# One-hot scatter in one-pass products, and the last block's down units at the head of the next pair

## The chip, the cores and the metric

The kernel runs on one core of one Trainium2 chip. The metric is the device time of one execution in microseconds (us), lower is better. Three runs of the kernel before gave a median of 1330.48 us, from 1329.83 to 1330.93.

## The reference

A two-layer transformer trunk for 256 tokens of width 1024, in float32. Each layer has a mixer (causal pooling and mLSTM heads), a layer norm, a channel mixer and another layer norm. The channel mixer of layer 0 is a dense SwiGLU; that of layer 1 picks two of eight experts for each token. The change lies in this last part:

```python
def moe_swiglu(x, w_router, b_router, wg, wu, wd):
    logits = (x @ w_router) + b_router
    top_v, top_i = lax.top_k(logits, 2)
    top_w = jax.nn.softmax(top_v, axis=-1)
    combine = jnp.sum(jax.nn.one_hot(top_i, 8) * top_w[..., None], axis=-2)
    out = jnp.zeros_like(x)
    for e in range(8):
        out = out + combine[..., e:e + 1] * ((silu(x @ wg[e]) * (x @ wu[e])) @ wd[e])
    return out
```

wg and wu are 1024 x 3584 per expert and wd is 3584 x 1024. All of them are read once: 336 MiB for this layer.

## The kernel before, in words

**Precision.** A matmul of float32 operands is two instructions in the trace; one of operands rounded to a short format (float32r) is one, called a one-pass matmul here. A product that has to be as exact as float32 is made of several one-pass matmuls: each weight unit is rounded by ScalarE into w_hi (L821) and VectorE writes the rest into w_lo (L1177). Tokens are split into high and low parts in the same way.

**Units.** The weights come as units of 128 x 2048 float32 (1 MiB), one DMA each on the sync engine's queue (SP), into a ring of nine slots (raw, arena and tokens memory). Four w_hi and three w_lo buffers follow. ScalarE rounds three units ahead of TensorE and VectorE subtracts two ahead, in the order of the units; a buffer comes free when TensorE is done with the unit in it (unit_done).

**Pairs.** The experts are sorted by their number of tokens and worked on in four pairs. In a pair, stream A is an expert with up to 128 tokens, and a unit of it costs 12 matmuls of 512 columns (three passes, `product`, L1768). Stream B is an expert with up to 64 tokens; its high and low parts stand side by side in one 128-wide operand, and a unit costs 8 matmuls (`one_pass`, L2098). B's lower rows are then added to the upper ones: ScalarE copies them to `fold` (L1059), TensorE adds them with a shift matrix (`add_lower`, L2145). The hidden width of 3584 is cut into blocks 0, 1, 2 of 1024 and block 3 of 512. A pair has 84 units: for each block b the gates (g), the ups (u) of A and B and then the downs (d) of the block before. In a pair, "units 16 to 19" are the downs of block 3 of the pair before (LATE = 4 units), placed behind the gates and ups of block 0 (ROUND = 20). The first pair starts at unit 4.

**Around a block.** After the gates ScalarE applies silu (L1043); after the ups VectorE multiplies (L1637); TensorE turns the product (L2132 for A, L2139 for B); ScalarE rounds it into eh_hi or eh_n (L1048, L1054) and VectorE writes the rest (L1643, L1650). The next block's gates of the same stream wait for that, because they use the same PSUM banks (2, 3 for A, 6, 7 for B). The dictionaries in `Events` say at which unit of the pair each step stands in each engine's queue.

**Gather and scatter.** TensorE gathers tokens by products with one-hot matrices (L2073), behind units 75 to 81. For the scatter, VectorE writes masks "token t sits in slot s" times the token's weight (L1520, L1531), TensorE turns them behind unit 68 (L2217) and ScalarE copies them to `scat` (L1109), in float32. When the last downs are through, ScalarE copies the sums of A (banks 0, 1) and B (banks 4, 5) to y_a (L1101) and y_b (L1104). `scatter_pair` (L2095, L2096) multiplies `scat` and y in float32, behind units 22 and 23, and VectorE adds the four results to `work` (L1633), behind units 24 to 27.

**Loops.** Pair 0 and pair 3 are written out. Pairs 1 and 2 are one body in a hardware loop on each engine (`Fori(1, PAIRS - 1)`). An overflow body (`extra`) for experts with more tokens stands behind a branch on n_over, which is 0 here.

**The end.** After pair 3 come its own four down units of block 3, the last scatter into banks 2, 3, 6, 7 (L2285, L2292), four additions (L1633), each followed by a bn_stats (L1729), the aggregates (L1733), two square roots on ScalarE (L1164) and the scaled result (L1742, L1744).

Of the kernel before, what the change touches and what calls it, by code (L numbers as in the profile page):

```python
# [7 lines left out]
F32 = mybir.dt.float32  # L8
# [24 lines left out]
E = 8  # L33
# [111 lines left out]
class Events:  # L145


    def __init__(self, order, first):
# [4 lines left out]
        self.turn_a = {(v + 4 if b < EXP_BLOCKS - 1 else v + 3): b for v, b in self.up_a.items()}  # L153
        self.turn_b = {(v + 4 if first and b == 0 else v + 5): b for v, b in self.up_b.items()}
# [3 lines left out]
        self.read_a = {after[0][(b - 1) % EXP_BLOCKS]: b for b in range(1 if first else 0, EXP_BLOCKS)}  # L158
        self.read_b = {after[1][(b - 1) % EXP_BLOCKS]: b for b in range(1, EXP_BLOCKS)}
        self.read_b[max(self.turn_b, key=lambda v: -self.turn_b[v])] = 0  # L160
        if first:
            self.read_a[max(self.turn_a, key=lambda v: -self.turn_a[v]) + 2] = 0
# [51 lines left out]
def build(nc, x, w_in, b_gates, conv_w, conv_b, pool_w, pool_scale, mlstm_g, w_out, ln1_g, ln1_b, ln2_g, ln2_b,  # L214
          wg_dense, wu_dense, wd_dense, w_router, b_router, wg_exp, wu_exp, wd_exp, consts, out):
    with ExitStack() as ctx:
# [16 lines left out]
        parts = sb("parts", [P, 3 * (XG + EH) + EBLK + TT * P + P + TT * NARROW], F32R)  # L233
# [25 lines left out]
        def carve(shape, start=None):  # L259
            if start is not None:  # L260
# [70 lines left out]

        esg = carve([EBLK], 2048)
        esg_n = carve([EBLK])
        y_a = carve([D])
        pickc, pickc_n = (shaped(y_a[:, n * TT * P:(n + 1) * TT * P], [TT, P]) for n in range(2))
        scat = carve([2, T])
        gt, eq = (shaped(scat[:, n, 0:TT * E * E], [TT, E, E]) for n in range(2))
        item_tab = carve([MAX_ITEMS + 1, 5])
        item_cur = carve([4, 5])

        y_b = carve([D])
        tables_end = at[0]
        logit = carve([TT, E], tables_end - D)
# [23 lines left out]
        assert at[0] <= tables_end  # L367
# [52 lines left out]
            shift_zero, fold_zero = map(sem, ("small_ready", "gatew_zero", "gatew_ready", "pool_steps", "convp_ready",  # L420
                                    "pool_ready", "mask_ready", "tokens_ready", "shift_zero", "fold_zero"))
        shift_ready, turn_go, sel_ready = map(sem, ("shift_ready", "turn_go", "sel_ready"))
        ln_last_in, ysb_half, mean_ready = map(sem, ("ln_last_in", "ysb_half", "mean_ready"))
# [170 lines left out]
        def _(sp):  # L594
# [71 lines left out]
            def later_loads(p, last=False):  # L666
                *late, a, b = (order_at(bass.ds(p * 2 + n, 1) if not last else slice(p * 2 + n, p * 2 + n + 1))
                               for n in range(4))
                pair_loads(p, PAIR, lambda stream, kind, blk, v: late[stream == "B"] if ROUND - LATE <= v < ROUND else
# [38 lines left out]
        def _(pool):  # L708
# [5 lines left out]
            g.memset(fold[0:NARROW, :].bitcast(F32), 0.0).then_inc(fold_zero, 1)  # L714
# [93 lines left out]
        def _(act):  # L808
# [304 lines left out]
            def extra(j):  # L1113

                i = j + PAIRS
                for n in range(2):
# [35 lines left out]
            a.copy(y_a, wide_bank(SUM_A, D)).then_inc(ysa_ready, 1)  # L1152
            act.wait_ge(unit_done, done(PAIRS, LATE - 1))
            a.copy(y_b[:, 0:HALF], bank[SUM_B]).then_inc(ysb_ready, 1)
# [13 lines left out]
        def _(dve):  # L1168
# [349 lines left out]
            def wide_slots(to, slot_of, combine_of):  # L1518
# [825 lines left out]
```

## Time and profile before

| | |
|---|---|
| median of three runs | 1330.48 us |
| the profiled execution, its own time | 1330.71 us |
| its span in the trace | 1328.9 us |
| TensorE, VectorE, ScalarE busy | 96%, 85%, 70% of the span |
| granted TensorE clock, mean | 0.992 of full speed |
| moved by DMA | 425.18 MB, 320 GB/s over the span |

The span is what the trace covers, from the first instruction to the last; the execution's own time has 1.8 us more. The expert layer runs from about 446 to 1310 us. TensorE is named PE for matmuls and PEld for weight loads, which overlap them; VectorE is DVE, ScalarE is ACT. Matmuls are pipelined, and a matmul's duration in the trace is longer than the distance to the next; the distance of the weight loads is the better measure of pace.

### The profile page before, as it was taken

What the parts mean: (1) busy time and instruction counts of PE and PEld (TensorE: products, weight loads), DVE (VectorE), ACT (ScalarE), POOL (GpSimd) and SP (SyncE); (2) the same over time, 40 slices, a digit from 0 to 9 for tenths busy, and PEclk for the clock granted to TensorE, in tenths of its full rate; (3) what the DMA queues carried; (4) which work ended last, traced back from release to release, by engine and by line L of the source; (5) the groups of instructions that cost most, each with busy time, mean ns of one, the idle gap of its engine ahead of it and who ended that gap; (6) DMA issues with size and microseconds to landing.
All of it is one profiled execution on the core that took longest, in us unless ns stands there. A gap on an engine that the chain in (4) does not pass through costs nothing.

```text
span 1328.9 us, 17008 instructions
## 1 busy us (share of the span) xinstructions
PE 1271.3 (96%) x6161; PEld 1035.8 (78%) x6161; DVE 1128.6 (85%) x943; ACT 929.7 (70%) x746; POOL 91.3 (7%) x111
## 2 busy tenths in 40 slices
PE   7999999999998999999999999899999999999996
PEld 6987888888977778778877777787777787677774
DVE  5887644458988899999998999888999989899997
ACT  5555334445543788888887888787878889788883
POOL 2560000000840000000000000000000000000000
PEclk9999999999998999999999999999999999999998
DMA  9647555544452999999999999999999999999992
GB/s 318 223 137 245 185 186 187 186 152 157 159 187 92 339 381 377 395 399 405 409 408 407 379 410 394 408 407 409 351 385 407 397 408 409 409 391 394 398 406 103
DMA packets 133053, 425.18 MB, mean 320 GB/s; under 512 B 9008, under 2 KB 11344, under 8 KB 132960
## 3 DMA queue, kind: packets, MB, share of 16 engines
q1 hardware_dynamic: 131600, 420.21, 83.3%
q0 software_dynamic: 1216, 3.71, 0.9%
q8 instruction: 53, 0.87, 0.3%
q14 instruction: 40, 0.33, 0.1%
q10 hardware_dynamic: 144, 0.07, 0.0%
HBM read 422.91 MB, written 1.05 MB: 319 GB/s over the span
## 4 chain that ended last, share of the span: by engine, by line
PE 74%; DVE 14%; issue 7%; ACT 4%; DMA 0%; DVEq 0%; ACTq 0%
PE bank L1770 19%; PE bank L1772 18%; PE bank L1771 18%; DVE w_lo L1177 8%; PE bank L2099 6%; PE bank L2100 6%; DVE w_lo L1191 2%; PE bank L2145 1%; ACT w_hi L836 1%; PE bank L2132 1%; PE bank L2073 1%; PE bank L2095 1%; PE bank L2096 1%; DVE arena L1272 1%; ACT w_hi L821 1%
## 5 line engine op out<-in xcount | busy, mean ns | idle before, releaser
L1177 DVE TENSOR_TENSOR w_lo<-raw,w_hi 128x2048 fp32r<-128x2048 f32 x216 | 485.9, 2285 | 34.4 <-PE bank L1772 18.7
L821 ACT CAST w_hi<-raw 128x2048 fp32r<-128x2048 f32 x216 | 407.5, 1915 | 67.6 <-PE bank L1772 66.7
L1770 PE MATMUL bank<-w_hi,parts 128*128 128x512 f32 x824 | 330.5, 401 | 18.7 <-issue 7.2
L1772 PE MATMUL bank<-w_hi,parts 128*128 128x512 f32 x824 | 322.8, 392 | 0.0
L1771 PE MATMUL bank<-w_lo,parts 128*128 128x512 f32 x824 | 322.7, 392 | 0.0
L2099 PE MATMUL bank<-w_hi,parts 128*128 128x512 f32 x672 | 270.9, 403 | 9.0 <-ACT arena L1043 3.1
L2100 PE MATMUL bank<-w_lo,parts 128*128 128x512 f32 x672 | 263.4, 392 | 0.0
L1770 PEld LDWEIGHTS bank<-w_hi,parts 128*128 128x128 f32 x824 | 155.7, 189 | 61.7 <-issue 19.5
L1191 DVE TENSOR_TENSOR w_lo<-raw,w_hi 128x2048 fp32r<-128x2048 f32 x61 | 140.7, 2308 | 60.0 <-PE bank L1772 45.5
L1177 DVE TENSOR_TENSOR w_lo<-arena,w_hi 128x2048 fp32r<-128x2048 f32 x80 | 181.1, 2285 | 9.4 <-issue 5.2
L1772 PEld LDWEIGHTS bank<-w_hi,parts 128*128 128x128 f32 x824 | 155.6, 189 | 33.4
L1771 PEld LDWEIGHTS bank<-w_lo,parts 128*128 128x128 f32 x824 | 155.8, 189 | 30.8 <-issue 0.7
L2099 PEld LDWEIGHTS bank<-w_hi,parts 128*128 128x128 f32 x672 | 126.7, 189 | 54.0 <-DVE w_lo L1177 23.0
L836 ACT CAST w_hi<-raw 128x2048 fp32r<-128x2048 f32 x61 | 115.9, 1909 | 75.2 <-PE bank L1772 66.1
L821 ACT CAST w_hi<-arena 128x2048 fp32r<-128x2048 f32 x80 | 150.9, 1913 | 17.5 <-PE bank L2100 14.1
L2100 PEld LDWEIGHTS bank<-w_lo,parts 128*128 128x128 f32 x672 | 126.8, 189 | 25.3 <-issue 0.7
L1177 DVE TENSOR_TENSOR w_lo<-tokens,w_hi 128x2048 fp32r<-128x2048 f32 x40 | 91.4, 2286 | 2.8 <-ACT w_hi L821 2.3
L1770 PE MATMUL bank<-w_hi,x_hi 128*128 128x512 f32 (+1 forms) x224 | 85.3, 381 | 4.0 <-DVE w_lo L1191 3.9
L1772 PE MATMUL bank<-w_hi,x_lo 128*128 128x512 f32 (+1 forms) x224 | 84.8, 378 | 0.0
L1771 PE MATMUL bank<-w_lo,x_hi 128*128 128x512 f32 (+1 forms) x224 | 84.7, 378 | 0.0
L821 ACT CAST w_hi<-tokens 128x2048 fp32r<-128x2048 f32 x40 | 76.9, 1921 | 6.0 <-issue 4.4
L1770 PE MATMUL bank<-x_hi,w_hi 128*128 128x256 f32 x256 | 73.5, 287 | 1.4 <-ACT arena L922 1.4
(256 smaller groups left out, 1255.4 us busy)
## 6 DMA issues: line engine op xcount, KB each, us to landing
raw<-in_wu_exp SPq DMA_DIRECT2D x76, 1024.0 KB, 10.8
raw<-in_wg_exp SPq DMA_DIRECT2D x70, 1024.0 KB, 10.0
raw<-in_wd_exp SPq DMA_DIRECT2D x70, 1024.0 KB, 10.6
arena<-in_wd_exp SPq DMA_DIRECT2D x29, 1024.0 KB, 10.2
arena<-in_wg_exp SPq DMA_DIRECT2D x26, 1024.0 KB, 10.9
arena<-in_wu_exp SPq DMA_DIRECT2D x25, 1024.0 KB, 9.1
raw<-in_w_in SPq DMA_DIRECT2D x20, 1024.0 KB, 5.8
tokens<-in_wg_exp SPq DMA_DIRECT2D x16, 1024.0 KB, 11.6
```

The lines of the kernel that those rows point to most:

```text
L821: a.copy(to, ring[s]).then_inc(hi_ready, 1)
L836: a.copy(w_hi[:, n % HIGH, :], raw[:, n % RAW, :]).then_inc(hi_ready, 1)
L1177: v.tensor_tensor(low(n), ring[s], high(n).bitcast(F32), ALU.subtract).then_inc(lo_ready, 1)
L1191: v.tensor_tensor(w_lo[:, n % SPLIT, :], raw[:, n % RAW, :], w_hi[:, n % HIGH, :].bitcast(F32), ALU.subtract).then_inc(lo_ready, 1)
L1272: ins = v.scalar_tensor_tensor(out=acc, in0=zqk[:, c, j:j + T], scalar=par_col(("conv_w", j), l, c), in1=acc, op0=ALU.mult, op1=ALU.add)
L1770: mm(psum, left[0], right[0], start=first, stop=False)
L1771: mm(psum, left[0], right[1], start=False, stop=False)
L1772: return mm(psum, left[1], right[0], start=False, stop=last)
L2073: last = mm(bank[n][:, kk * BOTH:(kk + 1) * BOTH], parts_[:, t, k * P:(k + 1) * P], pick_both[:, t, :], start=t == 0, stop=t == TT - 1)
L2095: mm(psum, scat[:, 0, at_t], y_a[:, at_d], start=True, stop=False)
L2099: mm(psum, left, right[0], start=first, stop=False)
L2100: return mm(psum, left, right[1], start=False, stop=last)
```

## The change

The one-hot matrix for the scatter no longer holds the tokens' weights, so it is exact in the short format. The weights are applied to the sums when they leave PSUM, together with the split in a high and a low part: ScalarE writes the high part with a scaled activation, VectorE the low part (`sums_low`). The factor per slot comes from four small products behind the turned masks (bank 7, copied to slot_w). The scatter has four one-pass matmuls per quarter instead of two float32 ones.

The parts lie in the memory of the last block's hidden values (eh_hi, eh_lo, eh_n) and of `fold`. So the last block's downs must have been multiplied before block 0 of the next pair writes there: they move from units 16 to 19 to units 0 to 3. Everything of block 0 moves four units back. Block 0's turn of A moves from behind unit 15 to behind unit 17 and is read there; its turn of B moves from unit 20 to unit 22. The scatter moves to units 6 and 7, the additions to 8 to 11. `add_lower` uses the lower 64 rows of its operands only, and the memset of the others goes. At the end the scatter is written without a branch in front of it, its B part by column halves, and VectorE's branch over the overflow body now stands behind the four additions and in front of the bn_stats.

```diff
-        for stream, kind, blk in (("A", "g", b), ("B", "g", b), ("A", "u", b), ("B", "u", b), ("A", "d", before),
-                                  ("B", "d", before)):
+        work = [("A", "g", b), ("B", "g", b), ("A", "u", b), ("B", "u", b)]
+        downs = [("A", "d", before), ("B", "d", before)]
+        for stream, kind, blk in work + downs if b else downs + work:
...
-        self.turn_a = {(v + 4 if b < EXP_BLOCKS - 1 else v + 3): b for v, b in self.up_a.items()}
-        self.turn_b = {(v + 4 if first and b == 0 else v + 5): b for v, b in self.up_b.items()}
+        self.turn_a = {(v + 2 if not first and b == 0 else v + 4 if b < EXP_BLOCKS - 1 else v + 3): b
+                       for v, b in self.up_a.items()}
+        self.turn_b = {(v + 5 if b else v + 4 if first else v + 3): b for v, b in self.up_b.items()}
...
-LATE_A, LATE_B = ROUND - LATE // 2 - 1, ROUND - 1
-SCATTER = {ROUND + 2: (0, 1), ROUND + 3: (2, 3)}
-ADD = {ROUND + 4: 0, ROUND + 5: 1, ROUND + 6: 2, ROUND + 7: 3}
+LATE_A, LATE_B = LATE // 2 - 1, LATE - 1
+SCATTER = {LATE + 2: (0, 1), LATE + 3: (2, 3)}
+ADD = {LATE + 4: 0, LATE + 5: 1, LATE + 6: 2, LATE + 7: 3}
...
+        ya_hi, ya_lo, yb_hi = (x.rearrange("p k c -> p (k c)") for x in (eh_hi, eh_lo, eh_n))
+        yb_lo = fold
...
-            g.memset(fold[0:NARROW, :].bitcast(F32), 0.0).then_inc(fold_zero, 1)
...
+            def sums_high(to, sums, n, ready):
+
+                a.activation(to, sums, ACT.Identity, scale=slot_w[:, n:n + 1]).then_inc(ready, 1)
...
+                        if b == 0 and not first:
+                            act.wait_ge(scat_mm, 4 * p)
                         lower_rows(b, 0)
...
                     if v == LATE_A and not first:
-                        a.copy(y_a, wide_bank(SUM_A, D)).then_inc(ysa_ready, 1)
+                        act.wait_ge(unit_done, done(p, v))
+                        act.wait_ge(slotw_ready, p)
+                        sums_high(ya_hi, wide_bank(SUM_A, D), 0, ysa_ready)
                     if v == LATE_B and not first:
                         act.wait_ge(unit_done, done(p, v))
-                        a.copy(y_b, wide_bank(SUM_B, D)).then_inc(ysb_ready, 1)
+                        sums_high(yb_hi, wide_bank(SUM_B, D), 1, ysb_ready)
...
+                        a.copy(slot_w[:], bank[7][:, 0:2]).then_inc(slotw_ready, 1)
                         a.copy(scat.rearrange("p a t -> p (a t)"), bank[3]).then_inc(scat_ready, 1)
...
+            def sums_low(to, sums, n, hi, rounded, ready):
+
+                dve.wait_ge(*rounded)
+                v.scalar_tensor_tensor(out=to, in0=sums, scalar=slot_w[:, n:n + 1], in1=hi.bitcast(F32),
+                                       op0=ALU.mult, op1=ALU.subtract).then_inc(ready, 1)
...
+                    if u == LATE_A + 1 and not first:
+                        dve.wait_ge(slotw_ready, p)
+                        sums_low(ya_lo, wide_bank(SUM_A, D), 0, ya_hi, (ysa_ready, p), yal_ready)
+                    if u == LATE_B + 1 and not first:
+                        dve.wait_ge(fold_mm, 2 * EXP_BLOCKS * p)
+                        sums_low(yb_lo, wide_bank(SUM_B, D), 1, yb_hi, (ysb_ready, p), ybl_ready)
...
-            dve.wait_ge(unit_done, done(PAIRS, LATE - 1))
-            v.tensor_copy(y_b[:, HALF:], bank[SUM_B + 1]).then_inc(ysb_half, 1)
+            dve.wait_ge(slotw_ready, PAIRS)
+            sums_low(ya_lo, wide_bank(SUM_A, D), 0, ya_hi, (ysa_ready, PAIRS), yal_ready)
+            dve.wait_ge(fold_mm, 2 * EXP_BLOCKS * PAIRS)
+            for n in range(2):
+                c = slice(n * HALF, (n + 1) * HALF)
+                sums_low(yb_lo[:, c], bank[SUM_B + n], 1, yb_hi[:, c], (ysb_ready, PAIRS + n), ybl_ready)
             n_over = dve.value_load(order_int[0:1, MAX_ITEMS + 2:MAX_ITEMS + 3], min_val=0, max_val=MAX_OVER)
+            for k, q in enumerate((0, 2, 1, 3)):
+                add_scattered(tail_mm, k + 1, q, bank[TAIL_BANKS[q]])
             with dve.If(0 < n_over):
...
-                mm(psum, scat[:, 0, at_t], y_a[:, at_d], start=True, stop=False)
-                mm(psum, scat[:, 1, at_t], y_b[:, at_d], start=False, stop=True).then_inc(scattered, 1)
+                mm(psum, scat[:, 0, at_t], ya_hi[:, at_d], start=True, stop=False)
+                mm(psum, scat[:, 0, at_t], ya_lo[:, at_d], start=False, stop=False)
+                mm(psum, scat[:, 1, at_t], yb_hi[:, at_d], start=False, stop=False)
+                mm(psum, scat[:, 1, at_t], yb_lo[:, at_d], start=False, stop=True).then_inc(scattered, 1)
...
+                        for n, picks in enumerate((pickc, pickc_n)):
+                            for t in range(TT):
+                                weights = mm(bank[7][:, n:n + 1], picks[:, t, :], item_cur[:, n, TT + t:TT + t + 1],
+                                             start=t == 0, stop=t == TT - 1)
+                        weights.then_inc(st_mm, 1)
...
-    nc = bacc.Bacc("TRN2", target_bir_lowering=False, num_devices=1, dynamic_dma_scratch_size=8192)
+    nc = bacc.Bacc("TRN2", target_bir_lowering=False, num_devices=1, dynamic_dma_scratch_size=4096)
```

## Rows read from the trace of the kernel before

**Rows 1.** The page, busy us by engine, with shares of the span.
```profile
PE 1271.3 (96%) x6161; PEld 1035.8 (78%) x6161; DVE 1128.6 (85%) x943; ACT 929.7 (70%) x746; POOL 91.3 (7%) x111
```
**Rows 2.** The page, the chain that ended last, by engine.
```profile
PE 74%; DVE 14%; issue 7%; ACT 4%; DMA 0%; DVEq 0%; ACTq 0%
```
**Rows 3.** Windows, units 0-27 of pairs 1-3: length, PE, PEld, DVE, ACT, POOL, clock, DMA, GB/s.
```profile
640.75:716.61 75.86, 74.61 (x318) 57.26 (x316) 67.72 (x37) 61.56 (x40) 0.00 (x0) 1.00 1.03 409
863.60:941.01 77.41, 76.14 (x316) 58.34 (x316) 65.60 (x35) 60.14 (x38) 0.00 (x0) 0.98 1.00 396
1084.48:1160.35 75.87, 74.43 (x318) 57.27 (x316) 67.91 (x37) 61.63 (x40) 0.00 (x0) 1.00 1.03 409
```
**Rows 4.** Timeline of weight loads: start, duration, and idle before with its releaser.
```profile
674.79 0.19 PEld L2099 LDWEIGHTS bank<-w_hi,parts 128*128 128x128 f32 x1 [0.41 <-DVE w_lo L1177]
...
678.72 1.03 PEld L2132 LDWEIGHTS bank<-cst,arena 128*128 128x128 f32 x8
...
690.59 0.19 PEld L1770 LDWEIGHTS bank<-w_hi,parts 128*128 128x128 f32 x1 [1.50 <-DVE w_lo L1177]
...
699.55 0.41 PEld L2095 LDWEIGHTS bank<-arena 128*128 128x128 f32 x2
...
702.78 0.19 PEld L1770 LDWEIGHTS bank<-w_hi,parts 128*128 128x128 f32 x1 [0.24 <-issue]
...
722.50 0.19 PEld L1770 LDWEIGHTS bank<-w_hi,parts 128*128 128x128 f32 x1
...
727.94 0.19 PEld L2099 LDWEIGHTS bank<-w_hi,parts 128*128 128x128 f32 x1
...
863.60 0.19 PEld L1770 LDWEIGHTS bank<-w_hi,parts 128*128 128x128 f32 x1 [3.56 <-issue]
...
1300.56 0.19 PEld L1770 LDWEIGHTS bank<-w_hi,parts 128*128 128x128 f32 x1 [0.58 <-issue]
```
**Rows 5.** The same timeline, around one tile's router products.
```profile
401.48 1.98 PEld L1779 LDWEIGHTS bank<-rout_w,arena 128*128 128x128 f32 x16
403.38 0.19 PEld L1770 LDWEIGHTS bank<-w_hi,parts 128*128 128x128 f32 x1
```
**Rows 6.** Timeline of VectorE in pair 1.
```profile
672.45 11.09 DVE L1177 TENSOR_TENSOR w_lo<-raw,w_hi 128x2048 fp32r<-128x2048 f32 x5
...
706.21 2.29 DVE L1177 TENSOR_TENSOR w_lo<-raw,w_hi 128x2048 fp32r<-128x2048 f32 x1 [3.87 <-PE bank L1772]
...
711.47 2.29 DVE L1177 TENSOR_TENSOR w_lo<-raw,w_hi 128x2048 fp32r<-128x2048 f32 x1 [2.37 <-PE bank L2100]
```
**Rows 7.** Waits of ScalarE, 446 to 1310 us, the longest.
```profile
ACT w_hi L821 <- PE bank L1772: 57.9, 70, 1.4
```
**Rows 8.** Windows of 30 us in pair 1, columns as in Rows 3.
```profile
735.00:765.00 30.00, 29.81 (x138) 23.72 (x137) 29.28 (x17) 24.30 (x16) 0.00 (x0) 1.00 0.99 375
...
795.00:825.00 30.00, 29.80 (x140) 23.77 (x139) 29.54 (x17) 24.36 (x18) 0.00 (x0) 1.00 1.04 393
```
**Rows 9.** Groups of instructions by form, 640 to 1300 us: busy, mean ns.
```profile
L1643 DVE TENSOR_TENSOR parts<-bank,parts 128x512 fp32r<-128x512 f32 x21 | 13.6, 684 | 5.9 <-ACT parts L1048 5.9
...
L1637 DVE TENSOR_TENSOR arena<-arena,bank 128x1024 f32<-128x1024 f32 x9 | 11.0, 1220 | 2.0 <-PE bank L1772 2.0
...
L1043 ACT ACTIVATE arena<-bank 128x1024 f32<-128x1024 f32 x9 | 9.2, 1027 | 17.6 <-PE bank L1772 17.6
```
**Rows 10.** Timeline of ScalarE, then of VectorE, at the end.
```profile
1310.58 1.28 ACT L1155 ACT_TABLE_LOAD   x1
1311.87 0.29 ACT L1155 ACTIVATE hstd<-small 128x1 f32<-128x1 f32 x1
1313.57 1.28 ACT L1164 ACT_TABLE_LOAD   x1 [1.40 <-issue]
...
1314.27 0.69 DVE L1633 TENSOR_TENSOR work<-work,bank 128x512 f32<-128x512 f32 x1 [3.60 <-PE bank L2292]
...
1319.87 0.21 DVE L1733 BATCH_NORM_AGGREGATE mv<-stats 128x2 f32<-128x12 f32 x1
```

More of the change, by code:

```diff
@@ L330, in build @@
         xg_n, eh_n = (shaped(parts[:, at_n + n * XG:at_n + (n + 1) * XG], [DK, P]) for n in range(2))
+        scat = shaped(parts[:, at_n + 2 * XG:at_n + 2 * XG + 2 * T], [2, T])
+        ya_hi, ya_lo, yb_hi = (x.rearrange("p k c -> p (k c)") for x in (eh_hi, eh_lo, eh_n))
+        yb_lo = fold
         esg = carve([EBLK], 2048)
         esg_n = carve([EBLK])
[L334 to L337, printed above, removed]
+        pickc, pickc_n = (carve([TT, P]) for _ in range(2))
+        gt, eq = (carve([TT, E, E]) for _ in range(2))
         item_tab = carve([MAX_ITEMS + 1, 5])
         item_cur = carve([4, 5])
-        y_b = carve([D])
-        tables_end = at[0]
-        logit = carve([TT, E], tables_end - D)
+        logit = carve([TT, E])
         rank = carve([TT, E])
@@ L668, in later_loads @@
                                for n in range(4))
-                pair_loads(p, PAIR, lambda stream, kind, blk, v: late[stream == "B"] if ROUND - LATE <= v < ROUND else
+                pair_loads(p, PAIR, lambda stream, kind, blk, v: late[stream == "B"] if v < LATE else
                            a if stream == "A" else b)
@@ L1723, in _ @@
                         extra(j)
-            def last_sums(t, n):
-                q = 2 * t + n
-                add_scattered(tail_mm, q + 1, q, bank[TAIL_BANKS[q]])
-                dve.wait_ge(acc_done, 4 * n_over + (4 * (PAIRS - 1) + q + 1))
-                st.add(v.bn_stats(stats[:, t, n, :], work[:, t, n * HALF:(n + 1) * HALF]))
+            dve.wait_ge(acc_done, 4 * n_over + 4 * PAIRS)
             def mean(t):
@@ L1748, in _ @@
                 for n in range(2):
-                    last_sums(t, n)
+                    st.add(v.bn_stats(stats[:, t, n, :], work[:, t, n * HALF:(n + 1) * HALF]))
                 mean(t)
@@ L2144, in add_lower @@
                 for hf in range(EXP_WIDTH[b] // HALF):
-                    last = mm(bank[WORK_B + hf], shift, fold[:, c0 + hf * HALF:c0 + (hf + 1) * HALF],
+                    last = mm(bank[WORK_B + hf], shift[NARROW:, :], fold[NARROW:, c0 + hf * HALF:c0 + (hf + 1) * HALF],
                               start=False, stop=True, skip_group_check=True)
@@ L2180, in start_block @@
                             pe.wait_ge(acc_done, 4 * p)
-                    elif stream == "B":
+                    elif stream == "A":
+                        pe.wait_ge(elo_a, p * FILLS)
+                    else:
                         pe.wait_ge(elo_b, EXP_BLOCKS * p)
@@ L2188, in pair @@
                     if q == 0:
-                        start_block(stream, kind, b, ROUND - LATE <= u < ROUND)
+                        start_block(stream, kind, b, u < LATE)
                     unit(u, done(p, u), stream, kind, b, q)
@@ L2216, in pair @@
                                 c = (n * TT + t) * P
-                                turned_slots = tr(bank[3][:, c:c + P], picks[:, t, :], ident)
-                        turned_slots.then_inc(st_mm, 1)
+                                tr(bank[3][:, c:c + P], picks[:, t, :], ident)
+                        for n, picks in enumerate((pickc, pickc_n)):
+                            for t in range(TT):
+                                weights = mm(bank[7][:, n:n + 1], picks[:, t, :], item_cur[:, n, TT + t:TT + t + 1],
+                                             start=t == 0, stop=t == TT - 1)
+                        weights.then_inc(st_mm, 1)
                     if u in GATHER and not last:
                         if GATHER[u] == 0:
+                            pe.wait_ge(slotw_ready, p + 1)
                             pe.wait_ge(scat_ready, p + 1)
@@ L2276, in _ @@
                 unit(v, done(PAIRS, v), "AB"[k], "d", EXP_BLOCKS - 1, q)
+            pe.wait_ge(scat_ready, PAIRS)
+            pe.wait_ge(ysa_ready, PAIRS)
+            pe.wait_ge(yal_ready, PAIRS)
+            for q in range(4):
+                t, n = divmod(q, 2)
+                for k, part in enumerate((ya_hi, ya_lo)):
+                    mm(bank[TAIL_BANKS[q]], scat[:, 0, t * P:(t + 1) * P], part[:, n * HALF:(n + 1) * HALF],
+                       start=k == 0, stop=False)
+            for n in range(2):
+                pe.wait_ge(ysb_ready, PAIRS + n)
+                pe.wait_ge(ybl_ready, PAIRS + n)
+                for t in range(TT):
+                    for k, part in enumerate((yb_hi, yb_lo)):
+                        last = mm(bank[TAIL_BANKS[2 * t + n]], scat[:, 1, t * P:(t + 1) * P],
+                                  part[:, n * HALF:(n + 1) * HALF], start=False, stop=k == 1)
+                    last.then_inc(tail_mm, 1)
             pe.wait_ge(table_ready, 1)
             n_over = pe.value_load(order_int[0:1, MAX_ITEMS + 2:MAX_ITEMS + 3], min_val=0, max_val=MAX_OVER)
-            def last_scatter():
-                pe.wait_ge(ysa_ready, PAIRS)
-                for q in range(4):
-                    t, n = divmod(q, 2)
-                    mm(bank[TAIL_BANKS[q]], scat[:, 0, t * P:(t + 1) * P], y_a[:, n * HALF:(n + 1) * HALF],
-                       start=True, stop=False)
-                pe.wait_ge(ysb_ready, PAIRS)
-                for q in range(4):
-                    t, n = divmod(q, 2)
-                    if q == 1:
-                        pe.wait_ge(ysb_half, 1)
-                    mm(bank[TAIL_BANKS[q]], scat[:, 1, t * P:(t + 1) * P], y_b[:, n * HALF:(n + 1) * HALF],
-                       start=False, stop=True).then_inc(tail_mm, 1)
-            with pe.If(n_over < 1):
-                last_scatter()
             with pe.If(0 < n_over):
+                pe.wait_ge(acc_done, 4 * PAIRS)
                 with pe.Fori(0, MAX_OVER) as j:
```

49 lines of the change are left out of this document (26 added, 23 removed).

## The prediction

> **What bounds the kernel now.** I read the page's shares first: TensorE is busy for 96% of the span, VectorE 85%, ScalarE 70% [rows 1]. The chain that ended last runs through TensorE for three quarters and through VectorE for 14% [rows 2], so the two take turns. The windows over the first 28 units of pairs 1, 2 and 3 say the same of the place that the change rebuilds: 75.86, 77.41 and 75.87 us, with TensorE busy nearly throughout and VectorE for 66 to 68 us [rows 3].
>
> The weight loads show the pace. Two units of stream A (24 matmuls) last from 722.50 to 727.94, 5.44 us, so 0.227 us a one-pass matmul: 2.72 us for an A unit (12), 1.81 us for a B unit (8) [rows 4]. VectorE makes a unit's remainder every 2.20 us: five take 11.0 us back to back [rows 6]. So TensorE sets the pace in A units and VectorE in B units, with three w_lo buffers between them. That is why B runs end in small stalls on w_lo (0.41 us at 674.79), and why the down units of block 3, placed behind block 0's, hold the largest: VectorE has block 0's product and remainders to do there, and TensorE waits 1.50 us at 690.59 [rows 4].
>
> The scatter is the other pause. A float32 matmul of 512 columns goes out as two instructions at 0.43 us each. Eight run from 699.55 to 702.78, with another 0.2 us before the next matmuls are at pace again, and that happens twice: 6.88 us a pair. VectorE then waits 3.87 and 2.37 us for a w_lo buffer [rows 4, 6].
>
> ScalarE never waits for a landing between 446 and 1310 us; its longest wait is for TensorE [rows 7]. But the stream is near its limit. It holds 409 GB/s where the ring always has a slot free, 375 in 735 to 765 and 393 in 795 to 825, where the rows of block 3 are half as long [rows 8]. A pair reads 84 x 1.0486 = 88.08 MB.
>
> **The change, part by part.**
>
> *One-pass scatter.* Per pair 16 instructions of 0.43 us (6.88 us with the restarts) become 16 one-pass matmuls, 16 x 0.227 = 3.62 us. Saved: 3.26 us in each of pairs 1 to 3.
>
> *Order.* I walk pair 1 from its start at 640.75 with 2.72, 1.81 and 2.20 us. TensorE's work in units 0 to 27 is 14 A units (38.1), 14 B (25.4), two folds (0.9), block 0's turns (1.03 for A [rows 4], about 0.6 for B with half the columns) and the scatter (3.62): 69.7 us. The stalls, unit by unit:
> - Units 0 to 6: the A downs take 5.44 us and the B downs 3.62, and VectorE keeps up. Its two new remainders of sums are 128x1024 reads of PSUM like the product of the gates, 1.22 us [rows 9]. The first ends before unit 5's remainder, which is then ready at about 652.9, while TensorE wants it at 652.5: 0.4 us. The second ends at 656.3, before the scatter wants it at 658.4.
> - Units 8 to 11 (B), with the four additions (128x512 reads of PSUM, 0.68 us as in the row of L1643 [rows 9]), begin after the scatter with full buffers: 0 to 0.2 us.
> - Units 16 to 19 (B): block 0's turn now stands behind unit 17. Its 1.0 us covers the stalls of units 18 and 19, but VectorE then reads the turned block (two of 0.68 us) before unit 20's remainder, which ends at 692.9 against 691.5: 1.4 us. This takes the place of 0.68 us in the run and 1.50 us in the downs.
> - Units 24 to 27 (B): 0.2 to 0.5 us, as in other B runs.
>
> Unit 28 then starts at about 712.4 instead of 716.61 [rows 3]: **4.2 us** saved in each of three pairs, 12.6 us, of which 3.26 x 3 = 9.8 is the scatter alone. Bounds: if the stalls only move, 9.8; if none is left, (75.86 - 69.7) x 3 = 18.5.
>
> *ScalarE.* Its two copies of the sums become scaled activations of the same shape, 1.03 us each by the silu's row [rows 9], plus a copy of two columns. It waits for units 1 and 3 before them, and behind it in its queue stand the roundings of units 5 to 7. After unit 1: 0.3 + 1.03 + 1.9 us to the rounding and 2.2 us to the remainder is 5.4 us, against 6.3 us until unit 5. The cover is unit 4; without it a microsecond a pair would show.
>
> *Weights by slot.* Four float32 products with one column each stand behind the transposes of unit 68, in all four pairs. The nearest row is the router's: 16 instructions with 8 columns from 401.48 to 403.38, 1.90 us, so 8 take 0.95 us [rows 5]. TensorE is the bound there. I take 0.9 x 4 = **3.6 us** lost; bounds 2 us (absorbed by a stall behind) and 4.
>
> *Nothing, and what covers it.* The multiplications dropped from the slot masks lie in VectorE's queue between remainders. The moved downs are the same four loads in the same ring slots, on SP's queue, with only the experts' order changed. The memset that goes is on GpSimd, busy for 7% of the span [rows 1]. The fold on 64 rows has the same 512 columns. The smaller scratch touches only GpSimd's early transfers. The scatter for the first pair does not exist.
>
> *Tail.* The last B unit ends at about 1309.8. Now the 16 scatter instructions follow, and VectorE's first addition is at 1314.27 [rows 10]. After the change the A part (1.8 us) runs while ScalarE rounds and VectorE subtracts B's sums in halves (0.6 us for ScalarE's first, then 0.68 us twice [rows 9]), so the first addition starts at about 1312.3, 2 us earlier, and the fourth at 1314.2. But VectorE's branch over the overflow body now stands between the additions and the first bn_stats. Before, it lay in the wait for the scatter. ScalarE takes the same branch behind its activation of L1155: the table load of that line starts at 1310.58, the activation ends at 1312.16, and the next table load, which waits for no engine, starts only at 1313.57 [rows 10]. So the branch costs 1.4 us if it waits for the activation's end and up to 3.0 us if the sequencer takes it at once. I take 2.8. Then the statistics begin at 1317.0, and their four plus two aggregates end near 1320.1, where the last aggregate ends now (1319.87 + 0.21). Tail: **0 us**; bounds -2.1 (branch free, as at a loop's exit) and +0.9 (the 3.56 us that TensorE idles at its loop's jump [rows 4]).
>
> The Trainium skill bears on this: "Runtime: NRT & Kernel Launch", section "Instruction fetch mechanics", says that a taken branch to a target outside the fetched pages stalls for a fetch. By that rule the tail gains nothing; by a free branch it would gain the 2.1 us. The trace agrees with it on ScalarE and on TensorE.
>
> *Stream.* Pairs 1 to 3 take 1300.56 - 640.75 = 659.8 us now [rows 3, 4], and 659.8 - 12.6 + 2.7 (their slots) = 649.9 us after: 216.6 us a pair. At 409 GB/s a pair's weights need 215.4 us, and 1.2 us more for the 30 us at 393: also 216.6. So the change uses up what room the stream has. The ring's nine slots keep it from showing at once. I add 0.5 us; bounds 0 and 7.5 (below).
>
> **Sum:** against the profiled execution, 1330.71 us (span 1328.9, 1.8 around it, 0.2 above the median): -12.6 + 3.6 + 0 + 0.5 = -8.5, so 1322.2; against the median of 1330.48, **1322.0 us**.
>
> **Rivals.**
> - *Stalls only move* (0.17): the turn in the middle of the B run costs what the old place cost. -9.8 + 3.6 + 0.5 = -5.7: 1324.8.
> - *The stream becomes the bound* (0.14): the 375 GB/s stretch stays. It costs 30 x 34/409 = 2.5 us a pair, 7.5 us in all, so the gain shrinks to about 2: 1328; with half of it recovered, 1325. For it: the equal 216.6 us. Against it: no wait for a landing now, and 375 stands where the ring was full after the long scatter.
> - *More is gained* (0.09): stalls mostly vanish and the branch is cheap: 1330.5 - 16 + 3.6 - 1.5 = 1316.5.
> - *VectorE is the bound; slower* (0.07): the time that it idles in the scatter (6.24 us) falls by the 3.26 that TensorE gives up, but it gets 2.5 us of new work a pair and stands 1.4 us in front of unit 20. If its other idle time is latency that cannot be used, pairs gain 0.8 and lose 1.4, and the slots cost 3.6: +5.4, 1336. It decides once VectorE's additions and waits take over 3 us a pair. For it: its 67.7 us of work in such a window [rows 3] grow to 70.2, of 71.7. Against it: that still fits, and the order of its queue was walked above.
> - *Scaled activations reload a table* (0.02): ScalarE would pay two loads of 1.28 us a pair, mostly covered: 1324.
>
> The likeliest case holds 0.51, with a range of its own of 1319.5 to 1324. A difference under 0.2% (2.7 us) cannot be told from no change here. Faster by more: 0.85; within: 0.07; slower: 0.08. The range that leaves out 2 in 10 reaches from the third rival to the second: 1317.5 to 1327.
>
> **What would show it.** The scatter's lines with 16 loads at 0.227 us each (3.62 us a pair), and VectorE's 3.87 and 2.37 us waits gone. Units 0 to 27 in 71 to 72 us, with a stall of 1 to 1.5 us in front of unit 20. Eight short matmuls at unit 68. In the tail, the first addition at 2 us after the last B unit, then a hole of 2 to 3 us before bn_stats. ScalarE without a wait for a landing. The prediction is wrong if that last wait appears in whole microseconds, if ScalarE's table loads grow, or if units 0 to 27 take over 74 us.

## The result, and the profile after

The changed kernel takes 1335.54 us (median of 7 runs, 1334.09 to 1337.15), the kernel before 1330.94 beside it. The ratio is 1.0031, with a 95% interval from 1.0022 to 1.0040: slower by 4 to 5 us, where the prediction said 1322.0 us, from 1317.5 to 1327. The profiled execution took 1335.99 us, 1334.2 of them in the span.

The page of the changed kernel, busy us by engine, and the chain that ended last:

```profile
PE 1274.2 (96%) x6193; PEld 1035.0 (78%) x6193; DVE 1137.6 (85%) x951; ACT 931.6 (70%) x751; POOL 90.8 (7%) x110
...
PE 72%; DVE 15%; issue 9%; ACT 4%; DMA 0%; DVEq 0%; ACTq 0%
```

Beside [rows 1] and [rows 2]: TensorE's matmuls were to be busy for less time, since 16 instructions of 0.43 us a pair became 16 of 0.227. They are busy for 3 us more, and "issue" grew from 7 to 9% of the chain. That points at TensorE itself, and not at another engine or a transfer.

The windows say where. First before, from the start of the last gather products in one pair to the same place a pair later (the last window ends where the downs left over from pair 3 start), columns as in [rows 3]:

```profile
636.22:855.55 219.33, 216.00 (x964) 170.32 (x962) 205.15 (x117) 181.86 (x131) 0.00 (x0) 1.00 1.02 402
855.55:1079.95 224.40, 217.91 (x964) 171.41 (x962) 205.24 (x117) 182.10 (x131) 0.00 (x0) 0.99 1.01 394
1079.95:1300.56 220.61, 216.83 (x956) 170.67 (x955) 207.91 (x115) 183.98 (x122) 0.00 (x0) 1.00 1.02 402
```

The same places after, and then units 0 to 27 of the three pairs, as in [rows 3]:

```profile
640.38:860.08 219.70, 216.84 (x972) 170.38 (x971) 207.67 (x119) 182.30 (x132) 0.00 (x0) 1.00 1.03 402
860.08:1085.16 225.08, 218.06 (x971) 170.08 (x970) 207.75 (x119) 182.38 (x132) 0.00 (x0) 1.00 1.01 392
1085.16:1306.14 220.98, 217.76 (x964) 170.77 (x962) 210.38 (x117) 184.17 (x123) 0.00 (x0) 1.00 1.02 398
...
644.91:718.18 73.27, 72.03 (x318) 56.96 (x316) 70.99 (x41) 61.22 (x40) 0.00 (x0) 1.00 1.03 408
866.78:943.35 76.57, 72.93 (x317) 56.67 (x317) 69.00 (x40) 59.73 (x38) 0.00 (x0) 1.00 1.00 383
1089.70:1163.09 73.39, 72.01 (x318) 57.00 (x316) 71.15 (x41) 61.29 (x40) 0.00 (x0) 1.00 1.03 409
```

Units 0 to 27 do gain: 2.6, 0.8 and 2.5 us. (Pair 2 opens behind the loop's jump, with two waits of over 2 us for w_lo.) Pairs 1 and 3 need 73.3 and 73.4 us, more than the 71 to 72 forecast, though less than the 74 named as a sign of being wrong. But whole pairs gain nothing: 665.76 us in all against 664.34. The rest of each pair gives back what its start saves. Another 4.2 us are lost before pair 1's window opens (640.38 against 636.22), and the end is 0.3 us shorter (28.06 against 28.34 us from the last window to the end of the span).

What gives it back stands in the timeline of the weight loads of pair 1. The scatter is as predicted, and so are the stalls in front of L1802:

```profile
657.18 0.18 PEld L1802 LDWEIGHTS bank<-w_hi,parts 128*128 128x128 f32 x1 [0.52 <-DVE w_lo L1192]
...
667.06 0.19 PEld L2127 LDWEIGHTS bank<-parts 128*128 128x128 f32 x1
...
668.87 0.19 PEld L2133 LDWEIGHTS bank<-w_hi,parts 128*128 128x128 f32 x1
...
697.70 0.19 PEld L1802 LDWEIGHTS bank<-w_hi,parts 128*128 128x128 f32 x1 [1.47 <-DVE w_lo L1192]
...
723.35 0.19 PEld L1804 LDWEIGHTS bank<-w_hi,parts 128*128 128x128 f32 x1
723.89 0.29 PEld L2179 LDWEIGHTS bank<-parts 64*128 64x128 f32 x2 [0.35 <-issue]
724.55 0.18 PEld L1802 LDWEIGHTS bank<-w_hi,parts 128*128 128x128 f32 x1 [0.37 <-issue]
724.65 0.19 PEld L1803 LDWEIGHTS bank<-w_lo,parts 128*128 128x128 f32 x1
```

Eight scatter loads take 668.87 - 667.06 = 1.81 us, twice a pair: 3.62. The last four lines are one place of the fold (L2179, the matmul that adds B's lower rows to its upper ones, now on 64 rows of weights). Before, the same place looks so:

```profile
721.82 0.19 PEld L1772 LDWEIGHTS bank<-w_hi,parts 128*128 128x128 f32 x1
722.04 0.41 PEld L2145 LDWEIGHTS bank<-parts 128*128 128x128 f32 x2
722.50 0.19 PEld L1770 LDWEIGHTS bank<-w_hi,parts 128*128 128x128 f32 x1
722.72 0.19 PEld L1771 LDWEIGHTS bank<-w_lo,parts 128*128 128x128 f32 x1
```

From the load in front of the folds to the second load behind them it was 722.72 - 721.82 = 0.90 us, with no idle time. Now it is 724.65 - 723.35 = 1.30 us: an idle 0.35 us in front and another 0.37 behind, of which the closer spacing of the loads gives some back. That is 0.40 us a place, and there are eight places a pair, 32 in all: 12.8 us. No wait for an engine is listed there ("issue").

### The profile page after: what moved, and what is told of

It is laid out like the page before. It is cut to its first block, busy times and chain, and to the rows that moved or that the text cites. A ratio compares the mean times of both kernels' runs of the same rounds, so it can differ in the third digit from the quotient of the medians.

```text
span 1334.2 us, 17112 instructions
## 1 busy us (share of the span) xinstructions
PE 1274.2 (96%) x6193; PEld 1035.0 (78%) x6193; DVE 1137.6 (85%) x951; ACT 931.6 (70%) x751; POOL 90.8 (7%) x110
## 4 chain that ended last, share of the span: by engine, by line
PE 72%; DVE 15%; issue 9%; ACT 4%; DMA 0%; DVEq 0%; ACTq 0%
PE bank L1802 19%; PE bank L1803 17%; PE bank L1804 17%; DVE w_lo L1192 8%; PE bank L2133 6%; PE bank L2134 5%; DVE w_lo L1206 2%; PE bank L2179 1%; ACT w_hi L839 1%; PE bank L2105 1%; ACT w_hi L824 1%; DVE arena L1287 1%; PE bank L2166 1%; PE bank L2090 1%; DVE parts L1662 1%
## 5 line engine op out<-in xcount | busy, mean ns | idle before, releaser
L1802 PE MATMUL bank<-w_hi,parts 128*128 128x512 f32 x824 | 332.9, 404 | 17.9 <-DVE w_lo L1192 7.7
L1802 PEld LDWEIGHTS bank<-w_hi,parts 128*128 128x128 f32 x824 | 155.6, 189 | 70.3 <-issue 21.7
L1802 PE MATMUL bank<-w_hi,x_hi 128*128 128x512 f32 (+1 forms) x224 | 85.1, 380 | 4.8 <-DVE w_lo L1206 4.8
L1802 PE MATMUL bank<-x_hi,w_hi 128*128 128x256 f32 x256 | 73.7, 288 | 1.4 <-ACT arena L925 1.4
```

The lines of the kernel that those rows point to most:

```text
L1802: mm(psum, left[0], right[0], start=first, stop=False)
```

## The experiments

My theory after this: weights with 64 rows cost TensorE a pause wherever they follow or precede weights with 128, and that price, 11 to 15 us, turned a gain of about 7 us into a loss. Rivals: VectorE with its new work, the new order or the slot weights cost more than forecast, and the fold's gaps only lie where a stall would have been anyway; or the price lies on each narrow matmul and not on the change between the two; or the gap has to do with the semaphores at these places. Ten runs were made, of nine kernels; each was timed in turns with the kernel before.

**The change without its narrow fold.**

```
-                    last = mm(bank[WORK_B + hf], shift[NARROW:, :], fold[NARROW:, c0 + hf * HALF:c0 + (hf + 1) * HALF],
+                    last = mm(bank[WORK_B + hf], shift, fold[:, c0 + hf * HALF:c0 + (hf + 1) * HALF],
```

(with the memset of fold's upper rows as before)

> The changed kernel with one part undone: the fold of B's lower rows is a product over all 128 rows again (and the memset of the upper rows is back). Theory FOLD: each 64-row fold costs about 0.5 us beside a 128-row one (the weight loads around it stop overlapping: 0.31 us before, 0.2 us within), 7 to 8 places a pair, some 15 us in all, so this kernel takes about 1320.5 us, close to the 1322 forecast. Rival VECTOR: VectorE sets the pace, with 2.5 us of new work a pair; the fold's gaps are then refilled by waits on w_lo and this kernel stays at 1333 to 1335.

Measured: 1323.8 us, ratio to before 0.9945 (0.9925 to 0.9965). Run once more in a later group:

> The changed kernel with the fold on 128 rows once more, as the base of the three runs beside it: 1323.8 us, within 1.5.

Measured: 1324.87 us, 0.9950 (0.9937 to 0.9962). The forecast of 1322.0 was right for this kernel to within 2 to 3 us: a gain of 6.9 and 7.0 us over the kernel before beside it, where 8.5 was forecast. Its windows, the same places as above, and units 0 to 27 of pair 1:

```profile
641.60:714.13 72.53, 71.12 (x318) 57.23 (x316) 70.89 (x41) 61.13 (x40) 0.00 (x0) 1.00 1.03 409
637.07:853.37 216.30, 213.27 (x972) 171.29 (x971) 207.38 (x119) 182.02 (x132) 0.00 (x0) 1.00 1.03 407
853.37:1075.18 221.81, 215.65 (x972) 172.19 (x970) 207.48 (x119) 182.14 (x132) 0.00 (x0) 0.99 1.02 400
1075.18:1292.92 217.74, 214.20 (x964) 171.66 (x962) 210.13 (x117) 183.61 (x122) 0.00 (x0) 1.00 1.03 406
```

The three pairs take 655.85 us, 9.9 less than with the narrow fold: 0.41 us for each of their 24 places. Before pair 1 it is 640.38 - 637.07 = 3.3 us, again 0.41 for each of pair 0's eight. Pairs 1 and 3 are the firm part (3.40 and 3.24 us for eight places each). Pair 2 differs between executions of one kernel: in the run once more it took 223.30 us instead of 221.81, while pairs 1 and 3 agreed within 0.03 us. Around the loop's jump, where TensorE idles, the mean granted clock over 20 us was 0.83 in that run (from 856.81 us) and 0.91 in this one (from 857.07); in the changed kernel it was 1.00 (from 860.38).

**The narrow fold alone, in the kernel before.** The same edit the other way round.

> The kernel before with one part of the change alone: the fold over 64 rows. FOLD: about 15 us slower than before, 1346 us. VECTOR: within 3 us of before.

Measured: 1341.17 us, 1.0089 (1.0063 to 1.0115), so 10.5 us by the medians and 12 by the ratio for the fold by itself, less than the 15 expected. By the traces the three pairs take 672.56 us, 8.2 more than before (0.34 a place), and pair 1 starts 1.3 us later. So the fold costs nearly as much without the new order, scatter and slot weights, which, with the run above, rules out the first rival. The fold's semaphores and waits are the same in both kernels. The folds' loads in pairs 1 to 3, by form (count, busy us, mean ns, idle us in front), here and in the kernel before:

```profile
L2145 PEld LDWEIGHTS bank<-parts 64*128 64x128 f32 x42 | 6.4, 184 | 8.5 <-issue 8.5
```

```profile
L2145 PEld LDWEIGHTS bank<-parts 128*128 128x128 f32 x42 | 7.9, 188 | 1.6
```

The load itself is no longer (184 ns against 188); it is the idle time that grows, and in front of it 8.5 us over 24 places is 0.35 us each. A reader who looks at durations alone finds nothing.

**One narrow matmul or two in a place.** On the change with the wide fold, the first matmul of each place is made narrow again and the second left wide.

```
-                    last = mm(bank[WORK_B + hf], shift, fold[:, c0 + hf * HALF:c0 + (hf + 1) * HALF],
+                    r0 = NARROW if hf == 0 else 0
+                    last = mm(bank[WORK_B + hf], shift[r0:, :], fold[r0:, c0 + hf * HALF:c0 + (hf + 1) * HALF],
```

(where the block has only one such matmul, at two places a pair, that one is narrow)

> The changed kernel with only the first matmul of each fold on 64 rows, the second (where the block is 1024 wide) on 128: 32 of the 56 fold matmuls are narrow, and every one of the 32 places still has one. Theory (the price is paid at each change of the row count, two a place): the same price as with all of them narrow, so 1335.5, within 2 us. Rival (the price is paid by each narrow matmul): 32/56 of 11.7 us above 1323.8, so 1330.5.

Measured: 1335.86 us, 1.0032 (1.0021 to 1.0043), the time of the changed kernel with all its folds narrow. The three pairs take 665.95 us against 665.76. A price on each narrow matmul would have given 1330.5. So the price is paid for each excursion from 128 rows to 64 and back, whatever number of matmuls it holds. The timeline of one place shows both changes:

```profile
680.03 0.18 PEld L2181 LDWEIGHTS bank<-parts 64*128 64x128 f32 x1 [0.35 <-issue]
680.45 0.19 PEld L2181 LDWEIGHTS bank<-parts 128*128 128x128 f32 x1 [0.24 <-issue]
```

**The turns of B, narrow all along.** The kernel before already had such places: the turn of B's product (L2139 before, L2173 after) loads 64 rows, eight times in a row (four in block 3). Here it takes 128 rows and columns, into both of B's banks.

```
-                    last = tr(bank[WORK_B][:, j * NARROW:(j + 1) * NARROW], esg_n[0:NARROW, j * P:(j + 1) * P],
-                              ident[0:NARROW, 0:NARROW])
+                    last = tr(bank[WORK_B + j // 4][:, (j % 4) * P:(j % 4 + 1) * P], esg_n[:, j * P:(j + 1) * P], ident)
...
```

(ScalarE and VectorE then read the turned product from its new columns.) On the change with the wide fold (and with the slot transposes behind unit 70, since they share a bank):

> The changed kernel with the fold on 128 rows, and the turns of stream B's blocks too as transposes of 128 rows (128 columns each instead of 64, into both of B's work banks; the slot transposes and weights go behind unit 70 instead of 68, since they share a bank). Theory (a change of the row count of TensorE's weights stalls it): the 0.31 to 0.35 us gap in front of each of the 16 turns of B goes, and eight turns take 1.0 us instead of 0.64 by the row of the turns of A, so the time is that of the kernel with the full fold alone, 1323.8, within 2 us. Rival (the gap belongs to the semaphore that TensorE raises in front of these turns, or to its wait there): the gap of 0.35 us stays, and the wider turns add 0.35 x 16 = 5.6 us, less what the stalls of the B runs take up: 1326 to 1329.

Measured: 1322.38 us, 0.9924 (0.9910 to 0.9938), and 1324.87, 0.9950 (0.9937 to 0.9962), for its base beside it. In the kernel before:

> The kernel before with the turns of stream B on 128 rows and nothing else. Theory (each change of the row count stalls TensorE): the 16 gaps of 0.35 us in front of these turns go (the 5.6 us of idle time put down to issue at that line), and the wider turns add 0.36 us each, so the time is unchanged to 1 us less, and 2.5 us less if the stall behind the last narrow turn counts too: 1328 to 1331. Rival (the gap is the semaphore's or the wait's): the gap stays, the turns are wider, up to 5.8 us more: 1333 to 1337.

Measured: 1331.95 us, 0.9999 (0.9989 to 1.0008). The loads of this line in the kernel before and in this one, from 600 us on:

```profile
L2139 PEld LDWEIGHTS bank<-cst,arena 64*128 64x128 f32 x88 | 6.5, 139 | 4.6 <-issue 4.6
```

```profile
L2139 PEld LDWEIGHTS bank<-cst,arena 128*128 128x128 f32 x88 | 10.4, 140 | 1.7
```

The gap went from every one of these places although their semaphores and waits are untouched. That rules out the third rival. One place, narrow in the kernel before and then wide:

```profile
749.92 0.19 PEld L2100 LDWEIGHTS bank<-w_lo,parts 128*128 128x128 f32 x1
750.46 0.58 PEld L2139 LDWEIGHTS bank<-cst,arena 64*128 64x128 f32 x8 [0.35 <-issue]
...
751.21 0.19 PEld L2100 LDWEIGHTS bank<-w_lo,parts 128*128 128x128 f32 x1
```

```profile
751.64 0.19 PEld L2100 LDWEIGHTS bank<-w_lo,parts 128*128 128x128 f32 x1
751.87 1.02 PEld L2139 LDWEIGHTS bank<-cst,arena 128*128 128x128 f32 x8
...
752.97 0.19 PEld L2100 LDWEIGHTS bank<-w_lo,parts 128*128 128x128 f32 x1
```

It is 1.29 us narrow and 1.33 wide: the loads grow by 0.44 us and the pause goes. (Four turns take 1.04 us narrow and 0.89 wide.) So the wide turns buy next to nothing, as the second run, with 11 executions, says. That the first run is 2.5 us under its base is not explained by its trace, where pair 1 takes 216.25 us against 216.30.

**The order alone.** The kernel before with the new order of units, turns and reads, its float32 scatter and wide fold kept.

```
-        for stream, kind, blk in (("A", "g", b), ("B", "g", b), ("A", "u", b), ("B", "u", b), ("A", "d", before),
-                                  ("B", "d", before)):
+        work = [("A", "g", b), ("B", "g", b), ("A", "u", b), ("B", "u", b)]
+        downs = [("A", "d", before), ("B", "d", before)]
+        for stream, kind, blk in work + downs if b else downs + work:
...
```

> The kernel before with the order alone (downs of block 3 first, block 0's steps, the scatter and the additions at their new units), the scatter still in float32. Walk of the prediction: 0.9 us a pair, 2.8 us faster in all, 1328 us. VECTOR: the turn inside the B run costs 1.4 us a pair more than it did, 1332 to 1335.

Measured: 1329.36 us, 0.9989 (0.9978 to 0.9999). Its windows of the three pairs:

```profile
634.63:853.20 218.57, 215.44 (x964) 170.46 (x963) 205.05 (x117) 181.88 (x131) 0.00 (x0) 1.00 1.03 405
853.20:1078.98 225.78, 218.01 (x963) 172.12 (x962) 205.40 (x117) 182.15 (x131) 0.00 (x0) 0.98 1.01 391
1078.98:1298.88 219.90, 216.30 (x956) 170.83 (x954) 207.74 (x115) 184.11 (x122) 0.00 (x0) 1.00 1.03 403
```

Pairs 1 and 3 gain 0.76 and 0.71 us; pair 2, with the loop's jump in it and a granted clock of 0.98, loses 1.4. The medians differ by 1.4 us. The run agrees with the direction, barely clear of the noise, and cannot tell 1.4 from the 2.8 us expected.

**Without the slot weights.** The change with the wide fold, slot_w filled with ones and the four products left out; this kernel leaves the tokens' weights out of the result.

```
-                        a.copy(slot_w[:], bank[7][:, 0:2]).then_inc(slotw_ready, 1)
+                        a.copy(slot_w[:], cst[:, C_ONES:C_ONES + 2]).then_inc(slotw_ready, 1)
...
-                        for n, picks in enumerate((pickc, pickc_n)):
-                            for t in range(TT):
-                                weights = mm(bank[7][:, n:n + 1], picks[:, t, :], item_cur[:, n, TT + t:TT + t + 1],
-                                             start=t == 0, stop=t == TT - 1)
...
```

> e1_fullfold without the four weight products a pair; slot_w is filled with ones, so the tokens' weights are left out of the result. If TensorE is the bound there, 0.9 us a pair, 3.6 us faster than e1_fullfold (1317 us by FOLD); if a stall behind absorbs it, 0 to 2 us.

Measured: 1322.19 us, 0.9948 (0.9929 to 0.9968). The median is 1.6 us under that of the kernel with them, where 3.6 was expected, but the ratios, 0.9948 and 0.9945, show no gain at all; and the traces of the two differ by 1.3 us in the hole behind VectorE's branch (next experiment). The products themselves do cost what was forecast; in the changed kernel, pair 1:

```profile
823.42 0.97 PEld L2258 LDWEIGHTS bank<-arena 128*128 128x128 f32 x8
824.31 0.19 PEld L1802 LDWEIGHTS bank<-w_hi,parts 128*128 128x128 f32 x1
```

824.31 - 823.42 = 0.89 us. Where the saving went is in the waits of ScalarE, 446 to 1310 us (us in total, times, longest), of the kernel without the products:

```profile
ACT w_hi L825 <- DMA arena<-in_wd_exp: 3.6, 6, 0.7
...
ACT w_hi L825 <- DMA raw<-in_wd_exp: 3.1, 5, 0.7
...
ACT w_hi L825 <- DMA tokens<-in_wg_exp: 1.6, 1, 1.6
...
ACT w_hi L825 <- DMA raw<-in_wu_exp: 1.6, 4, 0.9
```

These and two shorter rows make 10.4 us of waits for a landing, against 1.3 us with the products and none in the changed kernel. One of them can be followed to TensorE. The weights for the rounding at 828.55 us land late (0.72 us of idle time), ScalarE's silu stands behind that rounding, and TensorE's matmul waits 2.85 us for the silu. That wait, and below it the one at the same place with the products:

```profile
831.18 0.19 PEld L2134 LDWEIGHTS bank<-w_hi,parts 128*128 128x128 f32 x1 [3.26 <-issue]
```

```profile
831.29 0.19 PEld L2134 LDWEIGHTS bank<-w_hi,parts 128*128 128x128 f32 x1 [1.17 <-DVE w_lo L1193]
```

So the lead of 1.4 us with which pair 1 starts (635.71 against 637.07 us), and the 0.9 us of its own products, are gone 195 us later. The three pairs, without the 0.9 us of products in each, take 217.57, 222.19 and 217.10 us, 656.86 in all against 655.85. At this pace the stream of weights has become a bound. This rests on one trace.

**VectorE's branch moved.** On the change with the wide fold, the branch over the overflow body stands in front of the last two remainders of sums, where VectorE idles; both sides hold the remainders and additions.

```
+            def last_sums():
...
             with dve.If(0 < n_over):
+                last_sums()
                 with dve.Fori(0, MAX_OVER) as j:
...
+            with dve.Else():
+                last_sums()
```

> The changed kernel with the fold on 128 rows, and VectorE's branch over the overflow body in front of the last two remainders of sums instead of behind the four additions (both sides of the branch then hold the remainders and the additions). VectorE idles 1.91 us in front of those remainders, and the branch costs 2.8 to 2.9 us behind the additions (3.12 us of idle time in front of the statistics). If the fetch begins at the branch and lies in that idle time, the statistics follow the additions within 0.2 us and the remainders come up to 1 us late: 1.8 to 2.9 us less than 1323.8, so 1321 to 1322. If the fetch costs as much there as it saves behind (the body on the far side is another page to fetch): 1323.8.

Measured: 1322.49 us, 0.9931 (0.9919 to 0.9943), beside 0.9950 (0.9937 to 0.9962) for its base: 2.4 us less by the medians, with intervals that overlap a little, so the trace has to carry the reading. VectorE's timeline at the end, first with the branch in its old place and then moved:

```profile
1303.10 1.41 DVE L1677 SCALAR_TENSOR_TENSOR parts<-bank,slot_w,parts 128x512 fp32r<-128x512 f32 x2 [1.91 <-ACT parts L1069]
1304.74 2.48 DVE L1653 TENSOR_TENSOR work<-work,bank 128x512 f32<-128x512 f32 x4 [0.23 <-PE bank L2333]
1310.34 1.29 DVE L1782 BATCH_NORM_STATS2 stats<-work 128x6 f32<-128x512 f32 x2 [3.12 <-issue]
```

```profile
1303.45 1.41 DVE L1677 SCALAR_TENSOR_TENSOR parts<-bank,slot_w,parts 128x512 fp32r<-128x512 f32 x2 [2.58 <-ACT parts L1069]
1305.09 2.48 DVE L1653 TENSOR_TENSOR work<-work,bank 128x512 f32<-128x512 f32 x4 [0.23 <-PE bank L2339]
1307.60 1.29 DVE L1788 BATCH_NORM_STATS2 stats<-work 128x6 f32<-128x512 f32 x2
```

The hole of 3.12 us is gone, and the remainders wait 0.7 us longer than before: 2.4 us against this trace. The hole itself is no constant. In the trace of the same kernel run again it was 1.97 us, and against that one the gain is 1.3 us:

```profile
1310.48 1.29 DVE L1782 BATCH_NORM_STATS2 stats<-work 128x6 f32<-128x512 f32 x2 [1.97 <-issue]
```

The Trainium skill, "Runtime: NRT & Kernel Launch", section "Instruction fetch mechanics", says that a taken branch out of the fetched pages stalls for a fetch. The traces agree as to the stall: 2 to 3 us behind VectorE's branch, and less where the engine idles anyway. That it is a fetch, no row here shows.

**All three edits together** (wide fold, wide turns, branch moved).

> The changed kernel with all three edits: the fold on 128 rows, the turns of B on 128 rows, and VectorE's branch in front of the last remainders of sums. If the last two savings (2.5 and 2.4 us at the medians of their runs, each with an uncertainty as large) are real and add up: 1324.3 - 4.9 = 1319.5, range 1318 to 1321.5, ratio to before 0.9905. If the turns of B saved nothing (the gap of 0.35 us only changed into wider turns) and the 2.5 us were scatter between runs: 1322, the time with the branch alone.

Measured: 1320.82 us (5 runs, 1318.99 to 1321.58), ratio to before 0.9917 (0.9903 to 0.9930). It beats the kernel before by about 10 us and the changed one by about 15. It lies between the two expectations, 1319.5 and 1322, and its interval overlaps that of the kernel with the moved branch alone, so these runs do not show that the wide turns earn anything.

## Why the prediction was wrong

**The step that failed** is the sentence "The fold on 64 rows has the same 512 columns", which put the fold at nothing. The columns are the same and so is the load's duration. What changed is that 64-row weights stand between 128-row ones, and TensorE pauses at both changes: 0.41 us a place, 32 places, 13.2 us up to the end of pair 3's window in the two traces. The medians give 10.7 to 11.7 us (1335.54 against 1324.87 and 1323.8), and 10.5 in the kernel before. The spans differ by 12.1 us, 1.1 less than the 13.2, because the branch's hole was shorter in the changed kernel's trace (1.95 against 3.12 us).

The trace of before held the clue, in a place where the prediction read only a duration. Its loads for the turn of A and the turn of B, pairs 1 to 3:

```profile
L2132 PEld LDWEIGHTS bank<-cst,arena 128*128 128x128 f32 x84 | 9.9, 140 | 1.6
...
L2139 PEld LDWEIGHTS bank<-cst,arena 64*128 64x128 f32 x84 | 6.1, 139 | 4.2 <-issue 4.2
```

The same operation, once with 128 rows and once with 64, and only the second idles on "issue": 4.2 us in front of 12 runs of loads. Read as a price of 0.35 us for an excursion and multiplied by 32 places, this gives 11 us, and the forecast would have been 1333, a loss. The Trainium skill names a cost of this kind: "Mode switching requires drain: Changing tiling mode (not just tile) drains the TensorE" ("TensorEngine Tiling (Array Packing)", section "Key Properties"). The pauses at both ends of an excursion, 0.35 and 0.37 us, agree with that; the page gives no price and does not say that weights of 64 rows are such a change, and no row here shows that the pause is a drain. What makes TensorE pause stays open; that the change of rows brings the pause is shown.

The other steps, in the prediction's order:

- *One-pass scatter*, 3.62 us instead of 6.88: right, 1.81 us twice.
- *Order*, units 0 to 27 in 71.65 us with 0.4 us at unit 5, 1.4 us at unit 20: the walk had both stalls right (0.52 and 1.47 us). With the wide fold they take 72.53 us, 0.9 more than forecast, and 0.7 us more with two narrow places in them. The walk gave B's turn 0.6 us for its loads and nothing for the 0.35 us of idle time in front of them, the same omission as with the fold.
- The two together with the slot weights: -9.9 us forecast for three pairs, 655.85 - 664.34 = -8.5 measured. The sum is 1.4 us too large, half of it in pair 2 (-2.6 us, where -3.3 was forecast), and pair 2 differs by 1.5 us between two executions of this kernel.
- *ScalarE*: its scaled activations take 1.12 us instead of the 1.03 taken, and reload no table; no wait behind them shows.
- *Slot weights*, 0.9 us a place: right (0.89, and 0.85 us more until pair 1's window). Dropped, they give back 1.6 us by the medians and nothing by the ratios, below the lower bound of 2; the trace shows the stream setting the pace then.
- *Stream*, 0.5 us: no wait for a landing in the changed kernel, 1.3 us with the wide fold (216.3 us in pair 1), 10.4 us without the slot weights. The estimate of 216.6 us a pair as the place where it begins to bind was good: the pair that would have fallen below 216 took 217.57, and at 219.70 no such wait shows.
- *Tail*, 0 us: -0.3 in the changed kernel, +0.8 with the wide fold (1322.1 - 1292.92 = 29.18 us), both within the bounds, and the difference is the hole behind the branch. Its size, 2.8 us, was a fair choice; the traces have 1.84 to 3.12.

In all, with the wide fold: -8.5 + 0.85 + 0.84 = -6.8 us of span, where -8.5 was forecast. So the forecast's terms hold for this kernel, each to within 1.4 us, and the 1.7 us that are missing are mostly the pairs and the tail. The rival on the slower side (0.07) had the right sign and about the right time (1336), but by luck, for its mechanism is wrong: VectorE is busy for 71 of 73 us in units 0 to 27, but the same 71 us fit into 72.5 once TensorE's pauses are gone, and the pauses go and come with the rows of the weights alone.

## What to carry to other kernels

When a change touches the shape of a TensorE instruction, price the change of shape between neighbours and not only its own columns: sum the idle time on "issue" in front of every line whose rows differ from those around it. Narrowing one or two matmuls in a stream of full ones saved nothing here and cost 0.4 us for each excursion, while a run of eight narrow turns paid for its pause with shorter loads and no more. And a kernel within 1% of its stream's rate can give back what is shaved elsewhere.

## What the runs showed that was not expected

- Weights of 64 rows between those of 128, in the fold: 0.35 us of idle time in front and 0.24 to 0.37 behind, 0.40 us net, the same for one matmul as for two. Where a wait of 1.17 us for w_lo stood right behind the fold anyway, only 0.19 us net (1.88 us against 1.69 over such a place).
- Rows 64 to 127 (fold) and rows 0 to 63 (turn of B) cost the same in front; behind the turn of B the timeline lists no idle time.
- Eight transposes on 64 rows and columns take 1.29 us from load to load around them, on 128 rows and columns 1.33; four take 1.04 and 0.89.
- The hole behind a taken branch on VectorE differed between two executions of one kernel, 1.97 and 3.12 us. It is not shown what sets it.
